# Expert rows and gated rows turned by VectorE, input product in three blocks of 32 rows

## What is computed

```python
def _hier_moe(h, p):
    gl = (h @ p['w_group_router']).astype(jnp.float32)
    g_sel = one_hot(argmax(gl), N_GROUPS)            # top-1 group of 4
    ...
    top_v, top_i = lax.top_k(el_sel, TOP_K)          # top-2 experts of the 4 inside it
    ...
    for gi in range(N_GROUPS):
        a = jnp.einsum('bsd,edf->bsef', h, p['w_e1'][gi])
        b = jnp.einsum('bsd,edf->bsef', h, p['w_e3'][gi])
        y = y + jnp.einsum('bsef,efd->bsd', silu(a) * b * w_all[:, :, gi, :, None], p['w_e2'][gi])
    return y
```

## Time and profile before

| | |
|---|---|
| median of three runs | 2040.04 us |
| the profiled execution | 2054.78 us |
| its span, first to last instruction | 2053.0 us |
| TensorE matmul busy | 1966.6 us (96%) |
| VectorE busy | 698.5 us (34%) |
| ScalarE busy | 473.6 us (23%) |
| moved by DMA | 421.67 MB, 205 GB/s over the span |

### The profile page before, as it was taken

The page is one execution under the profiler, slowest core; times in us unless marked ns, Lnnn a source line. Parts: engine busy times, 40 slices in busy tenths (PEclk is TensorE's granted clock), DMA queues, the critical chain, the costliest instruction groups (busy, mean ns, idle before and its releaser), DMA issues.

```text
span 2053.0 us, 29144 instructions
## 1 busy us (share of the span) xinstructions
PE 1966.6 (96%) x12526; PEld 1064.7 (52%) x12526; DVE 698.5 (34%) x1669; ACT 473.6 (23%) x926; POOL 98.6 (5%) x135
## 2 busy tenths in 40 slices
PE   6989999999999989999989999999999998999996
PEld 3444556656655544444445565665665554444443
DVE  1293366333311131222223956633331113122223
ACT  2301234344200131011133133334420002111112
POOL 0000100100000010000020010010000001000002
PEclk9999999999999989999999999999999999999998
DMA  9777671321222549999952223132213243999993
GB/s 400 250 292 271 218 261 46 111 108 62 89 96 102 205 159 349 390 393 393 396 205 110 86 89 128 46 106 96 79 62 123 103 202 147 349 391 391 390 399 124
DMA packets 45168, 421.67 MB, mean 205 GB/s; under 512 B 5888, under 2 KB 6032, under 8 KB 18928
## 3 DMA queue, kind: packets, MB, share of 16 engines
q1 hardware_dynamic: 30240, 369.43, 46.5%
q0 software_dynamic: 8080, 26.78, 3.8%
q10 hardware_dynamic: 6720, 23.60, 3.2%
HBM read 389.08 MB, written 28.61 MB: 203 GB/s over the span
## 4 chain that ended last, share of the span: by engine, by line
PE 86%; DMA 8%; ACT 1%; DVE 1%; another core or an unknown queue 1%; issue 1%; POOL 1%; SPq 0%; POOLq 0%; ACTq 0%; DVEq 0%
PE psum L988 16%; PE psum L734 16%; PE psum L1092 9%; PE psum L1003 8%; PE psum L737 6%; PE psum L1113 6%; DMA pc<-we_in 5%; PE psum L1097 5%; PE psum L1034 4%; DMA ring<-wmod_in 2%; PE psum L652 2%; PE psum L828 2%; DMA ring<-wch_in 1%; PE psum L712 1%; PE psum L1108 1%
## 5 line engine op out<-in xcount | busy, mean ns | idle before, releaser
L734 PE MATMUL psum<-hT,ring 128*128 128x384 f32 x1088 | 367.2, 491 | 2.0 <-ACT pc L1270 1.9
L988 PE MATMUL psum<-hT,ring 128*128 128x384 f32 x1024 | 343.2, 488 | 0.0
L734 PEld LDWEIGHTS psum<-hT,ring 128*128 128x128 f32 x1088 | 203.0, 191 | 145.6 <-issue 18.7
L988 PEld LDWEIGHTS psum<-hT,ring 128*128 128x128 f32 x1024 | 192.1, 190 | 130.6
L1003 PE MATMUL psum<-pc,ring 128*128 128x384 f32 x512 | 175.6, 486 | 0.0
L2119 DVE TENSOR_TENSOR ytok<-pc,psum 128x384 f32<-128x384 f32 x32 | 17.7, 554 | 342.7 <-ACT pc L1525 342.7
L2111 DVE COPY scr<-psum 64x512 f32<-64x512 f32 (+1 forms) x180 | 91.9, 510 | 114.8 <-PE psum L1113 113.2
L1003 PEld LDWEIGHTS psum<-pc,ring 128*128 128x128 f32 x512 | 95.4, 190 | 61.5
L1720 DVE SCALAR_TENSOR_TENSOR pc<-pc,par 128x384 f32<-128x384 f32 x240 | 127.2, 611 | 0.0
L737 PE MATMUL psum<-ring,hT 128*128 128x512 f32 x288 | 125.8, 594 | 0.0
L1937 DVE TENSOR_TENSOR mva<-mva,psum 128x384 f32<-128x384 f32 x48 | 26.6, 554 | 282.4 <-PE psum L1003 263.4
(11 more groups left out here) (338 smaller groups left out, 2022.0 us busy)
## 6 DMA issues: line engine op xcount, KB each, us to landing
ring<-we_in SPq DMA_DIRECT2D x48, 2048.0 KB, 18.5
pc<-we_in SPq DMA_DIRECT2D x48, 2048.0 KB, 18.9
ring<-wmod_in SPq DMA_DIRECT2D x42, 1024.0 KB, 5.9
ring<-wch_in SPq DMA_DIRECT2D x18, 2048.0 KB, 8.6
ring<-wgate_in SPq DMA_DIRECT2D x16, 2048.0 KB, 8.1
ring<-wbr_in SPq DMA_DIRECT2D x16, 1024.0 KB, 8.0
ring<-wtok_in SPq DMA_DIRECT2D x6, 2048.0 KB, 8.3
expert_out_rows<-scr ACTq DMA_DIRECT2D x30, 384.0 KB, 9.5
```

The lines of the kernel that those rows point to most:

```text
L734: mm = pe.matmul(F[:, 0:T], wv[:, k, n * P:(n + 1) * P], hT[:, k, :], start=k == 0, stop=k == KD - 1)
L988: mm = pe.matmul(bank(5 + n % 2)[:, 0:T], wv[:, k, (n % 4) * P:(n % 4 + 1) * P], hT[:, k, :], start=k == 0, stop=k == KD - 1)
```

## The change

Four things change, all in the expert stage:

1. The rows of an expert are no longer turned by TensorE and copied by ScalarE. VectorE turns them from SBUF to SBUF with one instruction (`turn_rows`), which turns each square of 32 partitions by 32 elements in itself. So that squares suffice, the rows are loaded in another shape: four DMAs of 32 partitions, each with three pieces of 256 values (1 KB), fill all 128 partitions, and the token rows in `htok` hold feature n*8+k where k is the contraction step (`htok_k`; ScalarE writes them, and L1130 reads them, with a stride of 8 values).
2. The gated rows are turned by VectorE, too (`turn_hidden`), straight into `x_gT`. The hidden features come out in another order, for which the output weights are stored in plain order in HBM (partition p holds rows 4p to 4p+3, still 16 KB in one piece).
3. The input product runs in three blocks of 32 rows, each on four column tiles of 256 columns.
4. VectorE's order becomes turn_rows(e+1), open_hidden(e), keep_out(e-1), turn_hidden(e); ScalarE waits for the turned rows before it loads the next ones.

```diff
-        x_rows = [mva_flat[0:CAP, 512:1536], pc_flat[0:CAP, 12288:13312]]
+        x_rows = [mva_flat[:, 512:1280], pc_flat[:, 12288:13056]]
+        htok_k = htok.rearrange("p t (n k) -> p t k n", k=KD)
+        x_pre = psum[1][:, 0:6 * P].rearrange("p (a f) -> p a f", a=3)
...
-                def turn_rows(e):
-                    pe.wait_ge(rows_in[e % 2].sem, rows_in[e % 2].at(l, (e + 1) // 2 * 16))
-                    for k in range(KD):
-                        mm = pe.transpose(x_turned[:, k, :], x_rows[e % 2][:, k * P:(k + 1) * P], ident[0:CAP, 0:CAP])
-                    mm.then_inc(xt_done.sem, 1)
...
-                    for k in range(KD):
-                        for h in range(2):
-                            pe.matmul(bank(2)[BIG * h:BIG * h + BIG, :], x_h[:, k, 0:BIG], w[h][:, k, :],
-                                      start=k == 0, stop=k == KD - 1, skip_group_check=True)
-                    for k in range(KD):
-                        for c in range(4):
-                            part = slice(c % 2 * 256, c % 2 * 256 + 256)
-                            mm = pe.matmul(bank(3)[SUB * c:SUB * c + SUB, 0:256], x_h[:, k, BIG:CAP], w[c // 2][:, k, part],
-                                           start=k == 0, stop=k == KD - 1, skip_group_check=True)
+                    for b in range(CAP // SUB):
+                        for k in range(KD):
+                            for c in range(4):
+                                part = slice(c % 2 * 256, c % 2 * 256 + 256)
+                                mm = pe.matmul(x_pre[SUB * c:SUB * c + SUB, b, :], x_h[:, k, SUB * b:SUB * b + SUB],
+                                               w[c // 2][:, k, part], start=k == 0, stop=k == KD - 1,
+                                               skip_group_check=True)
...
-                def turn_hidden(e):
-                    pe.wait_ge(xg_ready.sem, xg_ready.at(l, e + 1))
...
-                        mm = pe.matmul(x_turned[:, k, :], htok[:, t, k * P:(k + 1) * P], first_pick[:, t * P:t * P + CAP],
+                        mm = pe.matmul(x_turned[:, k, :], htok_k[:, t, k], first_pick[:, t * P:t * P + CAP],
...
                     hidden(e)
-                    turn_rows(e + 1)
                     if e >= 1:
                         project(e - 1, 0)
                         project(e - 1, 1)
-                    turn_hidden(e)
...
-                    ac.dma_start(x_rows[e % 2], xs_d[e * CAP:(e + 1) * CAP, :]).then_inc(rows_in[e % 2].sem, 16)
+                    src = xs_d[e * CAP:(e + 1) * CAP, :].rearrange("(b i) n -> i b n", b=CAP // SUB)
+                    for q in range(P // SUB):
+                        ac.dma_start(x_rows[e % 2][SUB * q:SUB * q + SUB, :].rearrange("i (b c) -> i b c", b=CAP // SUB),
+                                     src[:, :, q * 256:(q + 1) * 256]).then_inc(rows_in[e % 2].sem, 16)
...
-                    if e + 1 < NE:
-                        copy_rows(e + 1)
                     if e < NE - 3:
+                        ac.wait_ge(xh_ready.sem, xh_ready.at(l, e + 2))
                         load_rows(e + 3)
...
-                    ac.wait_ge(xgt_done.sem, xgt_done.at(l, e + 1))
-                    ac.activation(mva_flat[:, 0:4 * CAP], bank(4)[:, 0:4 * CAP], ACT.Copy).then_inc(xgt_ready.sem, 1)
...
+                def turn_rows(e):
+                    ve.wait_ge(rows_in[e % 2].sem, rows_in[e % 2].at(l, (e + 1) // 2 * 64))
+                    ve.wait_ge(xab_done.sem, xab_done.at(l, e))
+                    ve.transpose(x_h.rearrange("p k (b i) -> p b k i", b=CAP // SUB),
+                                 x_rows[e % 2].rearrange("p (b j k) -> p b k j", b=CAP // SUB, k=KD))\
+                      .then_inc(xh_ready.sem, 1)
...
+                def turn_hidden(e):
+                    ve.wait_ge(xg_ready.sem, xg_ready.at(l, e + 1))
+                    if e >= 1:
+                        ve.wait_ge(xy_done.sem, xy_done.at(l, 2 * e))
+                    ve.transpose(x_gT.rearrange("p f (b i) -> p b f i", b=CAP // SUB),
+                                 x_g.rearrange("p b (j f) -> p b f j", f=4)).then_inc(xgt_ready.sem, 1)
+
                 for e in range(NE - 1):
+                    turn_rows(e + 1)
                     open_hidden(e)
                     if e >= 1:
                         keep_out(e - 1)
+                    turn_hidden(e)
                 keep_out(NE - 2)
                 open_hidden(NE - 1)
+                turn_hidden(NE - 1)
...
-        "we2": np.concatenate([_by_partition(inputs["w_e2"][l, e // EPG, e % EPG], D) for l in L for e in range(NE)]),
+        "we2": np.stack([inputs["w_e2"][l, e // EPG, e % EPG].reshape(P, -1) for l in L for e in range(NE)]),
```

## The result

| | before | after |
|---|---|---|
| median, runs taken together | 2040.43 us (2034.20 to 2041.99) | 2071.55 us (2064.07 to 2075.91) |
| ratio, 95% interval | 1 | 1.0147 [1.0123, 1.0171] |
| profiled execution, its span | 2054.78, 2053.0 us | 2075.91, 2074.1 us |

The change makes the kernel 31 us slower by the medians (30 by the ratio); the prediction was 2050.4 us, with a range of 2036 to 2066. The profile of before was an execution 14 us over its own median.

What follows compares the result with a forecast made beforehand. DMA, nearly balanced with TensorE, was taken to set the pace. Per layer -0.3 + 4.8 + 0.5 - 0.7 + 0.9 = +5.2 us, +10.4 for two, giving 2050.4 us against a median of 2040.04; range 2036 to 2066.

Steps and rivals of the forecast that it cites:

- strided weight loads: First-pick product, 48 weight loads of L1130: taken as 0, at most +9.2 us a layer if each takes twice as long.
- late landing: Row loads of the experts: rows are loaded three experts ahead, so a later landing by itself costs nothing.
- row load: Twelve loads a layer in the saturated stretch disturb the stream by +0.4 us each: +4.8 us, bounds -17 and +9.
- The bound: Expert stage: DMA, 18.0 us an expert at 394 GB/s, sets the pace over TensorE's 17.35 us.
- TensorE's train: TensorE's work per expert: 15.90 us instead of 17.35, 1.45 shorter, but no gain because DMA is already continuous.
- Start of the stream: From expert 0's Silu to expert 1's start: again 1.7 us; with shorter input products, -0.3 us (-0.6 to +0.6).
- VectorE's turns: VectorE's transposes: 0.96 us for 768 elements, 0.55 for 384, double if strided reads run at half rate.
- Rival D: Strided weight loads of L1130 run at half rate: at most 2069 us, half of that 2060; chance 0.12.
- After expert 14's weights: Expert 14's start to expert 15's product: 24.0 us against 23.4, with a 2.6 us wait; +0.5 us.
- Tail: Expert 15: input product -0.16, Silu to output product 1.8 us instead of 2.34; together -0.7 us.
- Clock: The 2.6 us gap before expert 14's output product may lower TensorE's clock, costing 1.76 us; even odds, +0.9.
- Signs: Right: steps of 18.2 to 18.8 us for experts 6 to 14; wrong: 18.0 or less, or first pick over 9 us.

Runs made afterwards that it cites:

- second profile: The kernel before, unchanged but for an empty line, run for a second profiled execution: 2040.97 us, ratio 1.0005, profiled span 2039.7 us.
- quarters beside the short train: Kernel before with three 32-row blocks, gated rows turned by VectorE, plain output weights, row load in four 256-column DMAs on 96 partitions: 2053.61 us, 1.0069.
- kernel with the short train: Kernel before with three 32-row blocks, gated rows turned by VectorE and plain output weights; old row load, rows turned by TensorE: 2047.21 us, 1.0036.
- kernel before with quarters: Kernel before with only its row load changed, to four DMAs of 256 columns (1 KB pieces) on 96 partitions: 2038.35 us, 1.0001.

## Why the prediction was wrong

The prediction had the way right and a third of the size. Its failed step is a term put at 0, the strided weight loads (14 us measured). Two more terms at nothing cost as well: a shorter train (7 us) and a late landing (the row load's part, which came near its forecast by luck).

**The bound: right.** A saturated stream sets the pace (second profile), and a train shortened by 0.73 us brings nothing (1.0036).

**TensorE's train: right.** Forecast 15.90, measured 15.81 us, and no gain from it. What I missed is that the shorter train isn't merely useless: it keeps the weight queue full, and with it the rows' queue short of turns. And three blocks with gated rows on VectorE alone, with the old load, cost 7 us (1.0036), mostly outside the stages and mostly unexplained.

**Start of the stream: right in sum, by luck.** Expert 0's start to expert 1's is 778.56 - 764.83 = 13.7 us, before 774.90 - 760.78 = 14.1: -0.4 for a forecast of -0.3. But that 14.1 holds an input product at the lower clock (8.78 us); in the second profile it took 7.09 and the distance is 12.4. Against this, after is 1.3 us later, 1.0 of it its own input product at a clock of 0.91 (11.55 us instead of 10.57).

**VectorE's turns: mis-sized.** 0.96 and 0.55 us were taken from copies, with the double left for strided reads; measured 1.58 and 0.92 us, and 0.98 and 0.58 without the stride. The base was right, and the stride's price came on top. It mattered because late rows put the turn on the chain.

**The strided weight loads: the step that failed.** I took 0 for them and bounded them at +9.2 us a layer; alone in the kernel before they cost 14 us (1.0067 [1.0050, 1.0083]), more than the whole forecast of +10.4. "No row shows a strided load" was a reason to take a value between the ends, not the lower end. Rival D, given 0.12, was thus true in its size, by luck, but not in its condition, loads at half rate: at the same clock they start every 0.240 instead of 0.213 us. The 192 ns of the earlier trace rows were those of the higher clock, and the 333 beside them, the longest, were those of the lower one; the strided product never leaves the lower one, and that is most of its price. The Trainium skill spoke against the change at this point ("SBUF — State Buffer", Door 1, the note on cachelines: reads that leave a 16-byte line pay). The trace agrees with 27 ns a load; the larger part came by the clock.

**The row load: near in size, wrong in mechanism.** I priced its disturbance of the stream, +0.4 us a load or 9.6 us for 24, and wrote that "rows are loaded three experts ahead, so a later landing by itself costs nothing". A load is issued two trains before its turn, 2 x 15.81 = 31.6 us, less the turn and four issues (1.6 and 1.3 us), and landed after up to 43.4 us. I counted 8 packets for each DMA engine; 384 pieces of 1 KB are 24. I had the landing of the old load (11.0 us) but did not ask what 35 packets instead of 14 do to it. The store behind the load went from 9.5 to 29.8 us, and in layer 1 it is the stores that are on the chain. The rate, which I priced, did not suffer against the old load (384 and 403 GB/s against 385 and 387). My nearest row for it was read wrongly: the copies of the earlier trace rows move pieces of 4 KB (their records show none of 1 KB).

What the new load costs in all is less than it looks in the chain, because weight blocks are the next wait: 4 to 8 us (taken out of after 1.0147 to 1.0126, or 7.6 us by the medians; quarters beside the short train 1.0036 to 1.0069). With late rows cured by 8 KB packets, 1.0040 with contiguous reads and this load stands against 1.0006 with the old load and TensorE turning the rows, 7 us; that these are the rate (380 to 392 against 386 to 399 GB/s) is likely but not shown, as the turns differ, too.

**After expert 14's weights: right.** Forecast a wait of 2.6 us and 24.0 us from expert 14's start to expert 15's; measured 2.77 us (1028.68), and 1036.97 - 1012.87 = 24.1 in layer 0. In layer 1 it was 30.6 us, since a late store held up VectorE.

**Tail: near.** Silu to output product 1049.46 - 1047.40 = 2.06 us, forecast 1.8, before 2.34.

**Clock: right in its condition, wrong in its place.** After the wait of 2.77 us, where I gave it even odds, the output product took 5.52 us, as without a wait. Slow products after a wait cost nothing where weight blocks set the pace (12.25 us in the kernel with the short train, stage unchanged). In after the waits are for rows, and the products after them took 12.25, 13.28, 12.54 and 12.48 us in layer 0, 9 us over 4 x 10.36; part of it comes on top.

**Signs.** I had named steps of 18.2 to 18.8 us, each released by a weight block. In layer 0 they are 15.8 us three and four times in a row and 18 to 24 us between, where VectorE was late. A first-pick product over 9 us was on my list of what would make the prediction wrong, for D; it came. That TensorE would wait for turned rows was on it, too, for every expert; it does for four in layer 0.

**What the difference of 31 us is made of.** Each part alone, by the ratios: the strided first pick 14 us (1.0067), three blocks with the gated rows on VectorE 7 us (1.0036), the row load's new shape 4 to 7 us. That is 25 to 28 of the 30 us. The parts overlap: taken out of after, contiguous reads bring 16 to 20 us, since a shorter turn of late rows counts too. So a split finer than that isn't to be had from these runs, and the 7 us of the second part are without a cause.

## What to carry to other kernels

When a transfer is cut into smaller pieces beside a saturated queue, count packets a DMA engine and per step in both queues: here they took turns one for one, and the queue that needed more turns than the other had packets fell behind at every step until TensorE stopped for it, however few bytes it moved. Cutting the big queue's packets in half cured it. Shortening an engine that isn't the bound is not free of risk: it removed the pauses in which the smaller queue caught up. And before a longer duration on TensorE is called the price of an access pattern, look at the granted clock in its window, and at what the same instruction takes without the pattern at that clock.

## What the runs showed of the hardware that was not expected

- Two queues on the same engines alternate one for one while both have packets waiting, 495 to 493 in 20 us, though one moves 16 KB and the other 1 KB at a time. In the kernel before with quarters it is 290 to 420 in 12 us.
- The shape of a load of 5% of the bytes moves the rate of all traffic: from 785 to 881 us, with 1 KB pieces on 96 partitions 403 and 408 GB/s, with 4 KB pieces on 96 partitions 379 to 394 (two profiles), with 1 KB pieces on 32 partitions 384 and 403, and with 4 KB pieces on 24 partitions 361 and 376 GB/s (the last beside a shorter train). Why smaller pieces disturb less is open.
- Strided f32 weight loads (a value each 32 bytes) start every 0.240 us and contiguous ones every 0.213 at a granted clock of 0.50. In the 12 strided products of 48 records here the clock never rose, in the 22 contiguous ones it always did.
- VectorE's turn of 768 f32 elements a partition in squares of 32 takes 1.58 us strided and 0.98 us contiguous.
